# Decode tokens' token projection on four side-by-side 32-column tiles of TensorE

## What is computed

```python
D_MODEL, SEQ, DEC_BATCH, DEPTH = 1024, 512, 8, 2
def layer_forward(x, pos, lw, conv_prefix, h0, paged):
    xn = rms_norm(x, norm1_g)
    z, xbc, dt_raw, q, k, v, iq, ik, iw, gate_a, gate_b = jnp.split(xn @ w_in, _in_offsets(), axis=-1)
    ...
    x = x + (mixed @ w_out).astype(x.dtype)
    x = x + peer_ffn(rms_norm(x, norm2_g), peer_wq, peer_keys, peer_u, peer_v).astype(x.dtype)
```

## Time and profile before

| | |
|---|---|
| median of the runs | 5554.57 us (5540.15 to 5554.66) |
| the profiled execution | 5553.32 us, of which the span in the trace 5551.6 us |
| TensorE, matmul | 4303.1 us busy, 78% |
| TensorE, weight load | 2639.8 us, 48% |
| VectorE | 3538.2 us, 64% |
| ScalarE | 1214.3 us, 22% |
| GpSimd | 2477.7 us, 45% |
| DMA | 1484.68 MB, 267 GB/s over the span |
| matmuls of the token projection (L689) | 607.7 us busy |

### The profile page before, as it was taken

One profiled execution on the slowest core, in us unless ns is written; L12 is line 12 of the kernel. 1 busy time (PEld: TensorE's weight loads), 2 busy tenths in 40 slices (PEclk: granted clock), 3 DMA queues, 4 the chain that ended last, 5 costly groups with the idle time before them and its releaser, 6 DMA issues. The chain is left out here.

```text
span 5551.6 us, 50287 instructions
## 1 busy us (share of the span) xinstructions
PE 4303.1 (78%) x15868; PEld 2639.8 (48%) x15868; DVE 3538.2 (64%) x7830; ACT 1214.3 (22%) x3036; POOL 2477.7 (45%) x2215
## 2 busy tenths in 40 slices
PE   7955886668678989589677786968778798767777
PEld 6334775543334766263344575553344476223333
DVE  4055648866678546686676868966668754844444
ACT  2042311121332112120432311121233211111111
POOL 0000010166455544546565333456655553577776
PEclk9975997689788999899898898988888899888888
DMA  4310641489788987789889876689878797799999
GB/s 142 117 62 29 236 151 43 150 282 346 261 274 270 328 291 271 276 307 375 289 299 319 322 247 221 204 295 341 300 261 278 269 360 264 258 371 409 409 409 360
DMA packets 583999, 1484.68 MB, mean 267 GB/s; under 512 B 60616, under 2 KB 251688, under 8 KB 581320
## 3 DMA queue, kind: packets, MB, share of 16 engines
q0 software_dynamic: 307200, 1115.82, 55.6%
q1 hardware_dynamic: 261272, 331.39, 18.0%
q10 hardware_dynamic: 15264, 34.26, 1.6%
HBM read 1435.37 MB, written 45.93 MB: 267 GB/s over the span
## 5 line engine op out<-in xcount | busy, mean ns | idle before, releaser
L2747 PE MATMUL duo<-vring,diag 128*128 128x512 f32 (+1 forms) x2976 | 1516.1, 660 | 397.0 <-DMA vring<-in_peer_v,eidx 169.0
L2619 POOL DMA_INDIRECT uring<-in_peer_u,eidx x981 | 1147.4, 1170 | 1117.6 <-DVE uring L2655 661.4
L2700 POOL DMA_INDIRECT vring<-in_peer_v,eidx x1024 | 1127.5, 1101 | 1035.9 <-PE duo L2747 471.8
L2747 PEld LDWEIGHTS duo<-vring,diag 128*128 128x128 f32 (+1 forms) x2976 | 593.9, 209 | 1199.9 <-issue 955.0
L2655 DVE SCALAR_TENSOR_TENSOR uring<-uring,xr 128x1024 f32<-128x1024 f32 x795 | 958.6, 1221 | 200.9 <-DMA uring<-in_peer_u,eidx 177.0
L689 PE MATMUL duo<-wx,xT 128*128 128x512 f32 (+3 forms) x1440 | 607.7, 580 | 32.2 <-PEq L133 32.1
L2780 DVE SCALAR_TENSOR_TENSOR x_tok<-vring,wt,x_tok 128x1024 f32<-128x1024 f32 x296 | 385.3, 1302 | 94.2 <-DMA vring<-in_peer_v,eidx 67.8
L2728 ACT ACTIVATE diag<-ident,wt 128x128 f32<-128x128 f32 x728 | 269.6, 395 | 742.0 <-PE duo L2747 677.9
L689 PEld LDWEIGHTS duo<-wx,xT 128*128 128x128 f32 (+1 forms) x1440 | 240.1, 178 | 387.1 <-issue 386.0
L2655 DVE SCALAR_TENSOR_TENSOR uring<-uring,duo 128x1024 f32<-128x1024 f32 x201 | 245.4, 1221 | 264.5 <-DMA uring<-in_peer_u,eidx 263.9
L533 PE MATMUL duo<-xT,wx 128*128 128x264 f32 (+1 forms) x1536 | 357.5, 397 | 36.6 <-ACT newcols L556 30.3
(11 more groups left out here) (471 smaller groups left out, 5262.4 us busy)
## 6 DMA issues: line engine op xcount, KB each, us to landing
wx<-in_w_in SPq DMA_DIRECT2D x32, 2048.0 KB
wx<-in_w_in SPq DMA_DIRECT2D x48, 1024.0 KB, 8.2
wm<-in_w_in SPq DMA_DIRECT2D x32, 1024.0 KB, 11.4
wm<-in_w_branch_a SPq DMA_DIRECT2D x32, 1024.0 KB, 11.2
wq<-in_peer_wq SPq DMA_DIRECT2D x32, 1024.0 KB, 7.8
tokm<-tout ACTq DMA_DIRECT2D x64, 256.0 KB
eb<-decays SPq DMA_DIRECT2D x32, 512.0 KB, 4.4
s_h<-in_state_ssm SPq DMA_DIRECT2D x32, 512.0 KB, 9.2
```

The lines of the kernel that those rows point to most:

```text
L2619: pool.indirect_dma_start(out=E.rings.urows[K % E.ur], out_offset=None, in_=table, in_offset=bass.IndirectOffsetOnAxis(ap=E.tiles[q][3][:, ...
L2700: pool.indirect_dma_start(out=E.rings.vrows[K % E.vr], out_offset=None, in_=table, in_offset=bass.IndirectOffsetOnAxis(ap=E.tiles[q][3][:, ...
L2747: mm = pe.matmul(G.bank[6 + c][0:m, :], G.diag[:, R % DR, 0:m], E.rings.vrows[K % E.vr][:, c * BANK:(c + 1) * BANK], start=first, stop=las ...
```

## The change

In the unit of the decode tokens (`j` = 2) each matmul of 8 stationary columns and `width` moving columns becomes four. Matmul `q` has 32 stationary columns (the last 32 of `G.xT`, 232 to 263: 24 prompt tokens and the 8 decode tokens), moves only the `q`-th quarter of the chunk's columns and writes to the output partitions 32q to 32q + 31. The decode tokens' results are the last 8 partitions of each group. ScalarE copies 128 partitions by a quarter of the width instead of 8 partitions by the whole, and stores with four DMAs instead of one; the counts on which the stores are waited for follow. Prompt units are as they were.

```diff
+    QUADS = 4
+    QROWS = P // QUADS
+    def parts_of(j):
+        return QUADS if j == 2 else 1
+    def stored(u):
+        return 16 * sum(parts_of(v % nt) for v in range(u % 2, u, 2))
...
-                    for k in range(KD):
-                        mm = pe.matmul(G.bank[u % 3][0:n, 0:width], G.xT[:, k, j * P:j * P + n], w[:, s, k, 0:width],
-                                       start=(k == 0), stop=(k == KD - 1))
+                    if j < 2:
+                        for k in range(KD):
+                            mm = pe.matmul(G.bank[u % 3][0:n, 0:width], G.xT[:, k, j * P:j * P + n], w[:, s, k, 0:width],
+                                           start=(k == 0), stop=(k == KD - 1))
+                    else:
+                        piece = width // QUADS
+                        for k in range(KD):
+                            for q in range(QUADS):
+                                mm = pe.matmul(G.bank[u % 3][q * QROWS:(q + 1) * QROWS, 0:piece], G.xT[:, k, 2 * P + n - QROWS:2 * P + n],
+                                               w[:, s, k, q * piece:(q + 1) * piece], start=(k == 0), stop=(k == KD - 1))
...
-                    dve.wait_ge(sem(f"stored{u % 2}"), 16 * (u // 2))
+                    dve.wait_ge(sem(f"stored{u % 2}"), stored(u))
...
-                        act.activation(out[0:n, u % 2, 0:width], G.bank[u % 3][0:n, 0:width], ACT.Copy).then_inc(sem("evac_a"), 1)
+                        m, piece = (n, width) if j < 2 else (P, width // QUADS)
+                        act.activation(out[0:m, u % 2, 0:piece], G.bank[u % 3][0:m, 0:piece], ACT.Copy).then_inc(sem("evac_a"), 1)
                     freed(act, u)
-                    act.dma_start(G.tokm[t * P:t * P + n, dc:dc + width], out[0:n, u % 2, 0:width]).then_inc(sem(f"stored{u % 2}"), 16)
+                    if j < 2:
+                        act.dma_start(G.tokm[t * P:t * P + n, dc:dc + width], out[0:n, u % 2, 0:width]).then_inc(sem(f"stored{u % 2}"), 16)
+                    else:
+                        for q in range(QUADS):
+                            act.dma_start(G.tokm[t * P:t * P + n, dc + q * piece:dc + (q + 1) * piece],
+                                          out[(q + 1) * QROWS - n:(q + 1) * QROWS, u % 2, 0:piece]).then_inc(sem(f"stored{u % 2}"), 16)
```

More of the change, by code:

```diff
@@ L713, in _ @@
                         if u >= 2:
-                            act.wait_ge(sem(f"stored{u % 2}"), 16 * (u // 2))
+                            act.wait_ge(sem(f"stored{u % 2}"), stored(u))
                         act.wait_ge(sem("acc"), u + 1)
-                        act.activation(out[0:n, u % 2, 0:width], G.bank[u % 3][0:n, 0:width], ACT.Copy).then_inc(sem("evac_a"), 1)
+                        m, piece = (n, width) if j < 2 else (P, width // QUADS)
+                        act.activation(out[0:m, u % 2, 0:piece], G.bank[u % 3][0:m, 0:piece], ACT.Copy).then_inc(sem("evac_a"), 1)
                     freed(act, u)
-                    act.dma_start(G.tokm[t * P:t * P + n, dc:dc + width], out[0:n, u % 2, 0:width]).then_inc(sem(f"stored{u % 2}"), 16)
+                    if j < 2:
[4 more added lines that the diff above has]
+                                          out[(q + 1) * QROWS - n:(q + 1) * QROWS, u % 2, 0:piece]).then_inc(sem(f"stored{u % 2}"), 16)
             nu = nc_ * nt
-            act.wait_ge(sem("stored0"), 16 * ((nu + 1) // 2))
-            act.wait_ge(sem("stored1"), 16 * (nu // 2))
+            for r in range(2):
+                act.wait_ge(sem(f"stored{r}"), stored(nu + (nu + r) % 2))
 def dt_vector(dve, sem, sp, dt, ad, raw, G, n):
```

## The result

The changed kernel takes 5499.49 us (median of 6 runs, 5487.08 to 5506.65), beside 5544.26 us for the kernel before (median of 6 runs, 5531.56 to 5554.66). The ratio is 0.9916, with a 95% interval of 0.9902 to 0.9930: some 47 us less (39 to 54). The two medians by themselves differ by 44.8 us. The profiled execution took 5499.34 us. The forecast was 5514 us, 40.0 us less than before, in a range of 5498 to 5530.

The account below looks back on a forecast made before the run. TensorE was taken to bound layer 0's stage, DMA gathers layer 1's. Layer 0: 41.2 - 0.3 - 0.9 = 40.0 us less, layer 1: 0; 5553.3 - 40.0 = 5513.3, plus 1.3, stated as 5514 us, range 5498 to 5530.

Parts of the forecast that it names:

- the level that the sum starts from: Whole kernel: profiled execution of 5553.3 us, taken as 1.3 us under the median of the runs.
- Two thirds of 20 us: Lower end of the range: layer 1's stage reaching two thirds of its at most 20 us gain, down to 5498 us.
- The term that was put at nothing: Layer 1's stage: 0 us gained, bytes unchanged and DMA share already 0.98; at best 20 us less.
- layer 1 gives too: Layer 1's stage: TensorE ahead keeps DMA queues full, nearing 409 GB/s; 5494 us at most, 5504 for half; chance 0.09.
- the 104-column unit: Last chunk's decode unit in layer 0: weight loads at 27 ns set the pace, 1.7 instead of 1.4 us, 0.3 us more.
- The store term: End of layer 0's stage: three more store issues of 0.29 us each on the path, 0.9 us more.
- L1440's burst: 16 passes of the wanted shape in the earlier trace, started within 0.37 us: taken to show four tiles run at once.
- The lower bound of 24.5 ns: Decode unit's pass-to-pass time from 0.37 us over 15 steps at L1440: a unit of 1.57 us, against 1.71 taken.
- half the overlap: Decode unit: weight load and move alternate, 54 ns per pass, 3.4 us per unit; 25 us less, 5530 us; chance 0.10.
- taking turns: Decode unit: tiles do not overlap, 64 passes at 107 ns, 6.9 us, nothing won; 5556 us; chance 0.07.
- slower: Decode unit: each weight load waits for the pass ahead, 134 ns per pass, 8.6 us per unit; 5573 us; chance 0.04.
- the 0.15 us of the prediction: Going from prompt unit to 8-column decode unit and back: some 0.15 us each way, left unchanged by the edit.

Follow-up runs that it names:

- the change of plan: Plan weight of layer 1's first-half token projection cut from 90 to 50, without and with the four tiles: that stage 181.9 and 154.2 us, ratios 1.0036 and 0.9888.
- the repeat: The changed kernel profiled and timed again with nothing altered: ratio 0.9934 (0.9913 to 0.9954) to the kernel before.
- single-tile kernel: Changed kernel with loops swapped and all four column quarters through one group of 32 output partitions: decode unit 7.17 us, layer 0's stage 179.0 us.

## Why the prediction was right in its mechanism and wrong in its sum

**The step that failed: the level that the sum starts from.** The sum is 5553.3 - 40.0, plus 1.3, and so starts from 5554.6 us, the median of three runs. With three more runs the same kernel has a median of 5544.26 us. Four other groups of 10 to 19 runs of it gave 5545.27, 5546.67, 5540.10 and 5533.39 us. So the first term was 10.3 us too high, and this is most of the 14.5 us by which 5499.49 lies under the forecast. The range had it wrong too. Two thirds of 20 us off 5514 is 5501, so only 3 of the 14 us by which the runs of before differ were left for the lower end of 5498. The result came out 1.5 us above this end, two of its six runs (5496.54 and 5487.08) lie below it, and by the ratio the time is 0.9916 x 5544.26 = 5497.7 us, just outside. Being inside by the median is luck.

**The term that was put at nothing: layer 1.** I took 0 "because the bytes are the same and the DMA share is already 0.98". It was some 4 us. The share of 0.98 in the earlier trace rows left room: 0.02 of 193 us is 3.9 us, and after the change the share is 1.00 and the rate 378 instead of 367 GB/s, for the same bytes. So the rival "layer 1 gives too" has a small part of truth. Why a TensorE that is ahead fills the DMA engines better was argued (it asks for weights earlier) and not tested. That gathers kept the rest of the gain away was shown by the change of plan: 27.7 us come out with fewer of them.

**Mis-sized: the 104-column unit.** I took 27 ns per weight load from L1802 as a limit on the row of loads as a whole, so that the unit would get 0.3 us longer. It got 0.8 us shorter: 0.75 instead of 1.52 us. On one tile the same unit took 2.21 us, (2.21 - 0.21)/63 = 32 ns per pass with its load, which is near the price I had. On four tiles it is 9 ns. The error was to apply one tile's price to four. The store term (0.9 forecast, 0.96 measured) was right.

**The change, added up again.** Eight units at 5.09 us (5.15 forecast) are 40.7 us. With 0.8 us for the 104-column unit and less 1.0 us for the stores this is 40.5 us in layer 0, and with 4 us in layer 1 some 44 to 45. The medians differ by 44.8 us; the ratio says 47 (39 to 54), and in the repeat 37 (25 to 48).

**Right, and shown.** Nearly all of the gain is layer 0's stage: 40.0 us forecast, 176.8 - 135.8 = 41.0 us in the first pair of traces, and 39.9 us between the shortest stage before (176.3) and the longest of the changed kernel (136.4). L1440's burst had told rightly that four tiles overlap, and the pace of 26.7 ns, a quarter of one pass's time, held over 64 passes (over whole rounds it is 109/4 = 27.3 ns). The lower bound of 24.5 ns was no other pace: L1440's 16 passes are four rounds of four, and its 15 steps hold only three of the long steps between rounds. The single-tile kernel excludes that the shape of the passes is the gain. The rivals "half the overlap" (54 ns), "taking turns" (107 ns) and "slower" (134 ns) were all excluded by the first timeline. The Trainium skill's rule (TensorE: Matmul & The Clock Gate, Part 3, The mechanism) that a weight load passes a running matmul only in another row group does not hold here: 64 loads and 64 passes of the same row group share 1.95 us.

**Also as forecast.** TensorE in layer 0 waits for no weights, stores or banks; its only idle time ahead of L699 there is the stage's start, 4.4 us in both kernels. In layer 1 the idle TensorE was granted less clock, as I had allowed for, and more so than I thought: 0.85 over the window, a mean of stretches at 2.4 and at 1.2 GHz, instead of 0.95. It needed 144.9 us there for what took 132.7 us in layer 0. Two prompt units show the price, one after a wait of 4.8 us and one without (granted clock 0.66 in 2536 to 2546 us, 0.99 in 2546 to 2556 us):

```profile
2540.07 10.12 PE L699 MATMUL duo<-wx,xT 128*128 128x512 f32 x16 [4.78 <-DVE tout L719]
...
2552.00 7.13 PE L699 MATMUL duo<-wx,xT 128*128 128x512 f32 x16
```

The slack covered this: TensorE was through 19.8 us before the stage's end.

## What to carry to other kernels

In these traces a unit with few stationary columns costs what its moving columns cost. Splitting those over four groups of 32 output partitions, with neighbouring matmuls on different groups, divided the pace from pass to pass by four at 128 and at 64 moving columns (a unit from 7.03 to 1.97 us with its switches). The order of the loop decides it: the same passes in the wrong order kept 5.95 of one tile's 7.17 us. Price such an edit stage by stage: the same 40 us of TensorE work were worth 41 us where it was busy 0.99 of a stage and about 4 us where the DMA engines were. A short burst of the wanted shape elsewhere in the trace tells beforehand whether tiles overlap, but a price taken on one tile is no price for four. And a forecast in absolute time is no better than its starting level: take it from more than three runs, or forecast the ratio. As a ratio this one was 5514/5554.57 = 0.9927, inside the interval measured.

## What the runs showed of the hardware

- Four column tiles reached the full factor of four at 128 moving columns (26.7 ns against 107 to 110 ns from pass to pass) and at 64 (13.8 ns), in float32. Four passes start 7 ns apart, and the next four 109 ns after the first of them.
- Switching between tile shapes costs no more than before: from the last pass of a prompt unit to the first of a decode unit it is 0.52 us in both kernels, where it is 0.43 inside the prompt unit, and on the way back 0.20 us, where one tile's passes are 0.11 us apart (before, 0.52 and 0.43). Each switch is some 0.09 us, less than the 0.15 us of the prediction.
- A narrow pass with its weight load also gets cheaper by nearly four on four tiles. With 26 moving columns they go by every 9 ns, against 32 ns on one tile, and with 8 stationary columns instead of 32 every 8 ns. What sets this floor is open.
- With all passes of a tile in a row there is still an overlap at each change of tile, worth between three and four passes (5.95 us against 7.17 us for the unit).
